# A two-block transformer kernel: x loaded transposed by the host, the first norm's token scale moved behind the products

## The reference, cut to what matters

```
a    = rms_norm(h, g_mix_pre)          # x * rsqrt(mean(x*x) + eps) * g
proj = a @ w_in                        # 2048 -> 5120
q, k, v = proj[:1024], proj[1024:2048], proj[2048:3072]
u    = proj[3072:] + b_glu             # value half, gate half
h    = u_value * sigmoid(u_gate)       # then a 31-tap convolution per channel
```

## Time and profile before

| | |
|---|---|
| Runs | 1823.80, 1823.88, 1824.35 us; median 1823.88 |
| Profiled execution, first to last instruction (span) | 1822.8 us; its own time outside of the span is not listed, the runs lie 1.0 to 1.5 us above the span |
| TensorE busy | 1803.1 us (99%) |
| VectorE busy | 1468.4 us (81%) |
| ScalarE busy | 902.7 us (50%) |
| HBM read | 421.23 MB, 233 GB/s over the span |

### The profile page before, as it was taken

How to read it: one execution, slowest core, us unless ns; L and a number is a source line. 1 busy time by engine, 2 the same in 40 slices (tenths; PEclk the granted TensorE clock), 3 DMA queues, 4 the chain that set the end, 5 groups by cost and what they waited for, 6 DMA issues and landing times.

```text
span 1822.8 us, 26157 instructions
## 1 busy us (share of the span) xinstructions
PE 1803.1 (99%) x9898; PEld 1560.7 (86%) x9898; DVE 1468.4 (81%) x1704; ACT 902.7 (50%) x1176; POOL 112.4 (6%) x217
## 2 busy tenths in 40 slices
PE   8999999999999999999999999999999999999998
PEld 7899988888888888888888888888888888888986
DVE  6899998878888897889887788755788778897854
ACT  6444566555335533553354557423656545445453
POOL 0000000000000000000000000001111010001000
PEclk9999999999999999999999999999999999999999
DMA  9756448777786787778977865654665784878562
GB/s 326 256 175 199 153 157 301 263 242 256 265 289 226 264 292 231 247 260 287 248 255 270 313 213 163 230 184 149 221 211 203 273 294 137 277 242 282 191 227 97
DMA packets 191017, 426.93 MB, mean 234 GB/s; under 512 B 12480, under 2 KB 12864, under 8 KB 189760
## 3 DMA queue, kind: packets, MB, share of 16 engines
q1 hardware_dynamic: 158560, 323.74, 52.3%
q0 software_dynamic: 27648, 100.68, 16.6%
q10 hardware_dynamic: 4704, 1.07, 0.3%
HBM read 421.23 MB, written 4.21 MB: 233 GB/s over the span
## 4 chain that ended last, share of the span: by engine, by line
PE 94%; DVE 3%; ACT 1%; issue 1%; DMA 1%; DVEq 0%; POOLq 0%; ACTq 0%
PE banks L2064 23%; PE banks L2109 14%; PE banks L2110 14%; PE banks L2111 14%; PE banks L2070 12%; PE banks L2055 4%; PE banks L2057 4%; PE banks L2056 4%; PE banks L2415 2%; PE banks L2431 2%; PE banks L2172 1%; PE banks L2406 1%; ACT w_hi L548 0%; DVE w_lo L1144 0%; DMA mod_raw<-in_ev_mod_w 0%
## 5 line engine op out<-in xcount | busy, mean ns | idle before, releaser
L548 ACT ACTIVATE w_hi<-raw 128x1024 fp32r<-128x1024 f32 x552 | 579.5, 1058 | 659.3 <-PE banks L2111 334.6
L1144 DVE TENSOR_TENSOR w_lo<-raw,w_hi 128x1024 fp32r<-128x1024 f32 x552 | 666.9, 1222 | 242.5 <-ACT w_hi L548 240.5
L2064 PE MATMUL banks<-a_pair,w_hi 128*128 128x512 f32 x1792 | 431.2, 391 | 1.6 <-DVE a_pair L1246 0.9
L2064 PEld LDWEIGHTS banks<-a_pair,w_hi 128*128 128x128 f32 x1792 | 328.3, 188 | 65.3 <-issue 2.2
L2109 PE MATMUL banks<-w_hi,b_hi 128*128 128x512 f32 x808 | 316.2, 391 | 0.2 <-DVE b_lo L1409 0.2
L2111 PE MATMUL banks<-w_hi,b_lo 128*128 128x512 f32 x808 | 314.5, 389 | 0.0
L2110 PE MATMUL banks<-w_lo,b_hi 128*128 128x512 f32 x808 | 314.4, 389 | 0.0
L1184 DVE SCALAR_TENSOR_TENSOR mod_sum<-mod_raw,silu_c,mod_sum 128x1024 f32<-128x1024 f32 x240 | 302.9, 1283 | 11.3 <-DMA mod_raw<-in_ev_mod_w 7.6
L2070 PEld LDWEIGHTS banks<-a_pair,w_lo 128*128 128x128 f32 x1792 | 230.2, 191 | 8.7
L2070 PE MATMUL banks<-a_pair,w_lo 128*128 128x256 f32 x1792 | 234.6, 283 | 0.0
L2109 PEld LDWEIGHTS banks<-w_hi,b_hi 128*128 128x128 f32 x808 | 151.7, 188 | 31.9 <-DVE b_lo L1409 0.6
(11 more groups left out here) (246 smaller groups left out, 1680.7 us busy)
## 6 DMA issues: line engine op xcount, KB each, us to landing
raw<-in_w_ff SPq DMA_DIRECT2D x128, 1024.0 KB, 6.6
mod_raw<-in_ev_mod_w POOLq DMA_DIRECT2D x96, 512.0 KB, 5.4
mod_raw<-in_od_mod_w POOLq DMA_DIRECT2D x96, 512.0 KB, 5.3
raw<-in_ev_w_in SPq DMA_DIRECT2D x40, 1024.0 KB, 5.2
raw<-in_w_in SPq DMA_DIRECT2D x39, 1024.0 KB, 5.2
raw<-in_od_w_in SPq DMA_DIRECT2D x32, 1024.0 KB, 5.8
raw<-in_w_out SPq DMA_DIRECT2D x16, 1024.0 KB, 6.3
raw<-in_ev_w_out SPq DMA_DIRECT2D x16, 1024.0 KB, 6.7
```

The source lines that it names most:

```text
L548: nc.scalar.activation(w_hi[:, s % SLOTS], raw[:, s // 2, KPS * (s % 2):KPS * (s % 2) + KPS, :], ACT.Copy).then_inc(hi_ready, 1)
L1144: nc.vector.tensor_tensor(w_lo[:, s % SLOTS], raw[:, s // 2, KPS * (s % 2):KPS * (s % 2) + KPS, :], w_hi[:, s % SLOTS].bitcast(F32), ALU.s ...
L2064: e = nc.tensor.matmul(out[:, f, :], w_hi[:, s % SLOTS, t, P * f:P * (f + 1)], rows[:, :, KPS * s + t, :], start=s == 0 and t == 0, stop=F ...
```

## The change

x is given a second time as `x_cols`, transposed on the host: feature on the partition, token along the row. SP loads it in five chunks (`X_CHUNKS`), in turn with u0's weights. ACT rounds x times the gain straight from SBUF (L682 of the new file), DVE takes the rest (L1340). The products of u0 use x without the token scale, and so do all ten blocks of w_in. ACT squares x in four pieces (L689), DVE adds the pieces (L1335, L1347, L1348), and two small products give the sum of squares of each token; root, reciprocal and diagonals follow, and one pair of products of ones by the diagonals spreads the scales over all partitions. ACT copies that row to `ln_rstd` (L692). TensorE waits for this copy before u1, whose accumulator lies in the same banks.

Behind the products the scale is applied: to the gate (L1389) and the value (L1395) by a further DVE multiply each, with the bias now added afterwards in four DVE operations of 128x256 (L1398) where one of 128x1024 stood; to q and k by DVE as they are read (`columns_scaled`, L1409), a read that ACT did before; to v by ACT (L721). The 13 warming products become 20, and they no longer wait for x. Two of the modulation parts move from u0 to the first feed-forward block.

```diff
-WARM = {0: 13, 1: 9, 2: 17, 4: 15}
+WARM = {0: 20, 1: 9, 2: 17, 4: 15}
+X_CHUNKS = [(0, 2), (2, 4), (4, 8), (8, 12), (12, 16)]
...
# SyncE
+            load_columns(0)
+            sp.dma_start(raw[:, 0, 0:KPS], W[:, 0:KPS, gate0]).then_inc(raw_first, 16)
+            load_columns(1)
+            sp.dma_start(raw[:, 0, KPS:2 * KPS], W[:, KPS:2 * KPS, gate0]).then_inc(raw_in[0], 16)
+            for q in range(1, 4):
+                load_columns(q + 1)
+                sp.wait_ge(split_done, 2 * q + 2)
+                sp.dma_start(raw[:, q], W[:, 4 * q:4 * q + 4, gate0]).then_inc(raw_in[q], 16)
             sp.dma_start(ident[:], io["ident"]).then_inc(ident_in, 16)
+            sp.dma_start(cols[:, KT:NCOLS], io["cols"][:, KT:NCOLS]).then_inc(cols_in, 16)
+            for n, c0 in enumerate((3072, 4096 + BW, 3072 + BW)):
+                load_block(BLOCK["u"] + n + 1, W, rows(), slice(c0, c0 + BW))
                 if n == 0:
                     sp.dma_start(quad[:], io["quad"]).then_inc(const_in, 16)
...
# ScalarE
+            nc.scalar.dma_start(cols[:, 0:KT], io["cols"][:, 0:KT]).then_inc(gain_in, 16)
             act.wait_ge(ones_ready, 1)
             load_root()
...
             for j in range(KT // 2):
-                norm_scaled(0, gain, a_hi, [j])
...
+                for k in (2 * j, 2 * j + 1):
+                    nc.scalar.activation(a_hi[:, k, :], x_cols[:, k, :], ACT.Copy, scale=gain[:, k:k + 1]).then_inc(norm_hi, 1)
+                act.wait_ge(raw_first if j == 0 else raw_in[j // 2], 16)
+                split_hi(0, [j])
+                if j in (1, 3, 4, 6):
...
+                    nc.scalar.activation(x_sq[:, 4 * c:4 * c + 4, :], x_cols[:, 4 * c:4 * c + 4, :], ACT.Square).then_inc(ssq_ready, 1)
+            root("mix")
+            act.wait_ge(rstd_row, 1)
+            nc.scalar.activation(ln_rstd[:], aux[:, 3, 0:T], ACT.Copy).then_inc(rstd_ready, 1)
+            act.wait_ge(cols_in, 16)
+            nc.scalar.activation(silu_c[:].rearrange("p a k -> p (a k)"), col("c", 0, 2 * KT), ACT.Silu).then_inc(silu_ready, 1)
...
# VectorE
+            for j in range(KT // 2):
+                for k in (2 * j, 2 * j + 1):
+                    dve.wait_ge(norm_hi, k + 1)
+                    nc.vector.scalar_tensor_tensor(a_lo[:, k, :], x_cols[:, k, :], gain[:, k:k + 1], a_hi[:, k, :].bitcast(F32),
+                                                   ALU.mult, ALU.subtract).then_inc(a_ready, 1)
+                split_lo(0, [j])
+                if j in (4, 5):
+                    add_squares(j - 3)
+                if j == 6:
+                    add_squares(3)
+                    link(nc.vector.tensor_tensor(x_sq[:, 0:2, :], x_sq[:, 0:2, :], x_sq[:, 2:4, :], ALU.add))
+                    nc.vector.tensor_tensor(sq_sum, x_sq[:, 0, :], x_sq[:, 1, :], ALU.add).then_inc(sq_summed, 1)
...
+                nc.vector.tensor_tensor(sig, wide_high[0], sig, ALU.add).then_inc(acc_free, 1)
...
+                nc.vector.tensor_tensor(sig, sig, rstd_b, ALU.mult).then_inc(u_summed, 1)
...
+                nc.vector.tensor_tensor(glu, wide_high[1], glu, ALU.add).then_inc(acc_free, 1)
+                dve.wait_ge(acc_free, 2 + ACC["u"] + 2 * i + 2)
+                link(nc.vector.tensor_tensor(glu, glu, rstd_b, ALU.mult))
                 dve.wait_ge(sig_ready, i + 1)
+                for f in range(FT):
+                    e = nc.vector.scalar_tensor_tensor(glu[:, f, :], glu[:, f, :], col("b_glu", FT * i + f), sig[:, f, :],
+                                                       ALU.add, ALU.mult)
...
+            def columns_scaled(n):
...
+                dve.wait_ge(step_done, 4 + 8 * (QKV + n + 1))
...
+                nc.vector.tensor_tensor(qk_T[:, HEADS * part + FT * half:HEADS * part + FT * (half + 1), :],
+                                        acc[n % 2][:, :].rearrange("p (f t) -> p f t", f=FT), rstd_b, ALU.mult).then_inc(acc_free, 1)
...
# TensorE
-            norm_product(0, BLOCK["u"], ACC["u"], wide_step, 3)
+            keep_warm(WARM[0])
+            for s in range(STEPS):
...
+                wide_step(BLOCK["u"], s, a_pair, wide_acc[0], tile_ready, None if s else low_ready).then_inc(step_done, 1)
+                if s == STEPS - 2:
+                    pe.wait_ge(sq_summed, 1)
+                    for tt in range(TT):
+                        e = nc.tensor.matmul(aux[:, 2, tt:tt + 1], sq_sum[:, P * tt:P * (tt + 1)], ones[:, 0:1], start=True, stop=True)
+                    e.then_inc(tok_summed, 1)
+            pe.wait_ge(scale_ready, TT)
+            for tt in range(TT):
+                e = nc.tensor.matmul(aux[:, 3, P * tt:P * (tt + 1)], ones[:], token_diag[:, tt, :], start=True, stop=True)
+            e.then_inc(rstd_row, 1)
+            pe.wait_ge(rstd_ready, 1)
```

More of the change, by code:

```diff
@@ L266, in build_program @@
         pair_tmp = sem("pair_tmp")
-        x_first = [sem(f"x_first{i}") for i in range(3)]
+        x_cols_in = [sem(f"x_cols_in{i}") for i in range(len(X_CHUNKS))]
+        gain_in = sem("gain_in")
+        sq_summed = sem("sq_summed")
+        tok_summed = sem("tok_summed")
+        glu_ready = sem("glu_ready")
         tile_done = sem("tile_done")
@@ L692, in _, with tokens_scaled @@
                 block_done(b + 1)
[L693 to L696 removed]
+                nc.scalar.activation(conv_in[:, FT * i:FT * (i + 1), PAD:HPAD], wide_low[1], ACT.Copy).then_inc(u_low_out, 1)
             QKV = BLOCK["qkv"]
[L699 to L701 removed]
+            def tokens_scaled(half):
+                n = 3 * half + 2
                 block_done(QKV + n)
[L703 to L708 removed]
+                act.wait_ge(acc_free, 2 + ACC["qkv"] + n)
+                for tt in range(TT):
+                    e = nc.scalar.activation(v_tok1[:, tt, BW * half:BW * (half + 1)], acc[n % 2][:, BW * tt:BW * (tt + 1)],
+                                             ACT.Copy, scale=norm_s[:, 6 + tt:7 + tt])
                 e.then_inc(acc_free, 1)
@@ L758, in head_slot1 @@
                         ahead1([6 * m + 4 + k])
-                        if m and k == 2 * m - 1:
-                            qkv_read(2 + m)
+                        if m == 3 and k == 5:
+                            tokens_scaled(1)
                 elif m < HEADS:
@@ L1366, in _ @@
                 dve.wait_ge(u_low_out, 2 * i + 1)
-                e = nc.vector.tensor_tensor(sig, wide_high[0], sig, ALU.add)
-                e.then_inc(u_summed, 1)
-                dve.wait_ge(u_summed, i + 1)
-                dve.sem_inc(acc_free, 1)
-                run_ahead(b + 1, each("ev_gate", 4, (1, 1, 1, 1)) if i == 0 else lambda m: conv_taps(7))
+                nc.vector.tensor_tensor(sig, wide_high[0], sig, ALU.add).then_inc(acc_free, 1)
+                if i == 0:
+                    dve.wait_ge(rstd_ready, 1)
@@ L1425, in head_slot1 @@
                             conv_taps(3 if k == 0 or m == 3 else 4)
+                        if m in (1, 2) and k == 2 * m - 1:
+                            columns_scaled(m + 2)
                         if k == 2 and m >= 2:
@@ L2058, in step_feature, with wide_step @@
                 return last
-            def wide_step(b, s, rows, out, tile_ready=None):
+            def wide_step(b, s, rows, out, tile_ready=None, low_ready=None):
                 def both(t):
```

135 lines of the change are left out of this document (58 added, 77 removed).

## The result

| | before | changed |
|---|---|---|
| Median of the runs | 1823.90 us (1823.80 to 1824.35) | 1835.02 us (1834.44 to 1836.25, four runs) |
| Ratio, 95% interval | | 1.0061 (1.0048 to 1.0073) |
| Profiled execution: span, own time | 1822.8 us | 1834.6 us, 1836.25 us (the slowest of its four) |

The changed kernel is slower by 11.1 us. The forecast was 1829.6 us with a range up to 1832.5: the sign was right, the size was not, and the measured time lies outside of the range. Two slow runs beside the experiments, of 1899.39 us (`before_extra`) and 2574.18 us (the kernel before), are not compared with the others. The profiled execution of the changed kernel is the slowest of its four, and the four times go roughly with the mean granted clock: 0.995 at 1836.25 and 1835.39 us, 0.997 and 0.996 at 1834.64 and 1834.44.

What follows compares the result with a forecast made beforehand. TensorE, busy 1803 of 1822.8 us, was taken as the bound. Earlier u1 -4.15, clock dip +2.65 and waits for VectorE +7.2 gave +5.7: 1828.5 us profiled, 1829.6 for the median, range 1820.5 to 1832.5.

Steps and rivals of the forecast that it cites:

- part 1: Program start: warming products no longer wait for x, so u0 starts at 8.1 us, 6.2 us earlier.
- part 2: End of u0: VectorE has more to do per step than TensorE, so u0 ends at 31.9 us, bounds 30.8 and 34.
- part 3: Gap ahead of u1: a chain of 4.95 us behind u0, so u1 starts at 36.85 against 41.0, 4.15 won.
- part 4: Gap ahead of u1: the clock falls to half and stays there for 5.3 us, +2.65 us, bounds 0 and +5.3.
- part 5: Behind the products: VectorE's added operations make TensorE wait 7.2 us, 3.7 of it by Q0 step 4; bounds 0 and 10.8.
- The 0.3 us in hand: Step 4 of u3: VectorE's `w_lo` ends at 96.17, TensorE starts the step at 96.5, so 0.3 us are spare.
- Q1 to Q5: four reads, 5.0: Attention blocks: four reads add 5.0 us to a full VectorE; after absorbed waits, 3.5 us of TensorE waiting.
- Its own sign: Prediction wrong if 80 to 250 us has no `w_lo` waits or waits sum under 4 us, or u1 starts before 35.
- part 5, end: First feed-forward block: two modulation parts moved there, 2.5 us over 61 us of products, cost nothing.
- The first rival: Behind the products: VectorE hides its additions; 1822.4 us with the clock dip, 1819.7 without; chance 0.12.
- no dip: Gap ahead of u1: the clock does not fall, everything else as forecast, 1827.0 us; chance 0.22.
- The constants come late: Ahead of u1: the wait for constants is last, 1 to 2 us behind the other chain, 1831 to 1832; chance 0.10.

Runs made afterwards that it cites:

- before_extra: Kernel before, with two extra 128x1024 VectorE operations of 1.24 us each between the second gate's sum and its sigmoid; 1827.68 us.
- read4_early: Changed kernel with VectorE's scaled read of block Q4 placed two splits earlier; 1829.94 us.
- warm_gap: Changed kernel with 16 warming products on TensorE between the scale products and u1; 1833.7 us.
- warm_slot: Changed kernel with twelve warming products in front of the scores of head 4; 1832.59 us.
- start_alone: Changed kernel without the scaling of gate, value, q and k, with reads and bias as in the kernel before; 1824.13 us.
- splits_first: Changed kernel with u1's splits ahead of the token scale, Q4's read two splits earlier, u3's step 4 and 5 roundings ahead of the second gate's sigmoid; 1821.18 us.
- no_multiplies: Changed kernel without the two multiplies by the token scale behind each gate and value block (5.0 us of VectorE); 1831.31 us.
- consts_later: Changed kernel with VectorE's wait for the small constants, and two small operations, moved behind u1's first four splits; 1835.44 us.

## Why the prediction was right about the sign and wrong about the size

- **Start of u0 (part 1).** Right: first wide product at 8.01 us, forecast 8.1.
- **End of u0 (part 2).** Right in kind, 0.95 us too early. The scale products start at 32.96 where the forecast implied 32.0. VectorE goes without a pause, and TensorE waits 0.5 us for it ahead of step 7, as forecast. The delay was there already at step 4, whose `w_lo` ended at 19.4 in place of 18.5. The chain shows where it comes from: the quarter of weights for steps 2 and 3 landed at 12.5, and the chain goes on from it over ACT and VectorE. TensorE also waited 1.1 us at 15 us for it. Up to and with this load SP had issued 3.1 MB, but by 12.5 us some 3.8 MB had been moved (168, 385 and 401 GB/s in the three stretches of 5 us), so later loads had been moved in part before it was complete. The forecast counted bytes as if loads landed strictly in turn.
- **The gap ahead of u1 (part 3).** Order and durations right: copy 33.60, table load 34.01, Silu 35.30, `w_hi` 35.44. The Silu follows the start of the table load by 1.29 us, as in the kernel before; the 2.66 us of the Trainium skill ("ScalarE: Activation LUTs", What ACT_TABLE_LOAD costs) do not show here either. The tie that I called between this chain and the constants was broken by 0.6 us in this trace: the constants landed last, 5.2 us after their issue as forecast, but that issue had slipped with `w_lo` of step 7. In `read4_early` it was a tie. u1 starts at 38.59, forecast 36.85: won 2.4 in place of 4.15.
- **The clock (part 4).** Right in kind and, partly by luck, in size. Forecast 2.65, measured 2.2 by u1's products against those of warm_gap. The 5.3 us were taken from the slow products at the program's start, where the granted clock reads 1.00 all the same; nothing tied that length to a dip inside the program. In the profiled execution products ran at half clock for 4.9 us. In `read4_early` the same place had a shorter dip, 24 products of u1 in 5.4 us against 6.1 here and 3.8 in warm_gap, so it cost 1.6 there.
- **VectorE up to Q0 (part 5).** Right: waits of 1.6 and 1.5 us at the two places named, forecast 2.0 and 1.7. The 0.3 us in hand was 0.4 in before_extra. At Q4 the sum of all this was forecast as +2.2 (-4.15 + 2.65 + 3.7) and is +3.8.
- **The step that failed** is the last line of part 5, "Q1 to Q5: four reads, 5.0", priced at 3.5 us of waits for `w_lo`. It counted the reads as work that makes the splits late, in a VectorE with under 0.3 us in hand, and nothing else. Both halves were wrong. First, the splits never made TensorE wait there: behind Q0 the changed kernel has no wait for `w_lo` up to 250 us, and three reads made TensorE 0.14 us later. VectorE did fall back, but had room to: its split of 221.91 us starts at 227.60, 5.7 us later, where TensorE is 3.8 later. Second, `columns_scaled` also releases what the scores wait for (`acc_free`), and the forecast gave that nothing. ACT, which did these reads before, read Q4 at 227.3, and the scores of head 4 came at 231.94. In VectorE's program the read stands behind three splits and twelve taps and came at 238.4. The cost is a wait of 3.8 us, and since TensorE then stands still, the clock falls a second time: 2.4 us by warm_slot. With small waits behind, 7.1 us arose between Q4 and the feed-forward block, where the forecast had 3.5 from Q1 on. The forecast had seen what the clock does behind a gap, but applied it to one gap alone.
- **Its own sign.** It named a sum of waits under 4 us between 80 and 250 us as a sign that it is wrong. The waits for `w_lo` there are 3.1 us, and only the wait for the read, which it did not have, brings the sum to 6.9. So that the total looks near the forecast 7.2 us is luck.
- **The modulation parts (part 5, end)** and all that follows were priced at nothing. The distance grows from 11.0 at 360 us to 11.8 at the end. The traces show about half of it: a wait for `w_lo` of 0.24 us at 1008 that the kernel before does not have, and one of 1.37 at 1079 that was 1.16. Which operation makes them late was not tried.
- **The first rival**, that VectorE hides its additions, fell: in start_alone, without them, the time is 1824.1; with them it is 1835.0. The case "no dip" fell as well, by the trace. "The constants come late" held in kind, by 0.6 us where it had 1 to 2.
- **Small slips in the sums.** Step 4 of u3 starts at 96.7 by the chain's rows and not at 96.5, which is why 0.4 us were in hand there. The forecast's own bounds, added up, give about 1826.7 to 1832.3, not 1827.5 to 1832. Neither changes the account.

The range failed for one reason: it let each known cost vary within its bounds and held no case in which a moved read is waited for. Its own text says that VectorE "is full" from Q1 on. To ask of every operation moved there who waits for it would have found the scores.

What is open: what makes the 0.8 us behind the first feed-forward block, why a dip is longer in one execution than in another, and whether a further gain lies in the 1.0 us that splits_first still waits at Q0. The early start itself is worth up to 7.2 us (u1 at 33.8 against 41.0), of which splits_first keeps 2.9.

## What to carry to other kernels

When an operation moves to another engine, list what it releases as well as what it costs: its new place is behind everything that the new engine's program has ahead of it, and the waiter pays for all of that. An idle gap on TensorE costs more than its length, because the clock can be at half behind it (3.8 us of waiting and 2.4 of clock here); one gap closed or one instruction moved was worth more here than 5 us of work left out. An engine that is busy without a pause may still hold idle time of its own: look at what its splits wait for before taking work away from it, since work merely moved later came back as other waits.

## What the hardware did that I had not expected

- Half clock after a short wait. In before_extra TensorE idled for 2.04 us up to 98.64, and the granted clock was 0.71 and then 0.50 in the next stretches. The waits of 1.4 to 1.8 us in the changed kernel and six of its variants had the clock at 1.00 behind them in every profile. With waits of 3.8 us and of 4.4 to 5.4 us it fell each time.
- The dip is not of one length, at the same place of the same program. At u1 the changed kernel's profile is at half clock from 36.7 to 43.5 us, with products from 38.59; `read4_early` has 1.00 from 36 to 38 us, 0.57 and 0.58 in the next two stretches of 2 us, and 1.00 again from 42, with products from 37.75. So the fall can also come after the products have resumed. At the scores of head 4 the dip cost 2.4 us in the changed kernel and 1.6 in `no_multiplies` and `consts_later`, each counted over the next 28 products against those of warm_slot. Differences of that size would explain much of the spread of the runs, but the executions without a profile do not show it.
- Loads issued close together do not land strictly in turn. The first 1 MB load of weights had 9.22 us in the chain, and more had been moved by then than was issued up to it. The 5.2 us of the earlier trace rows are the median of the whole page; over the first 60 us of the kernel before such a load took 8.6.
